# A two-layer hybrid decoder step: one load for the parameters, an earlier up branch in the last chunk, and a final norm by tile

## The reference

```
def rms_norm(x, g):
    y = x * rsqrt(mean(x * x, axis=-1) + EPS)
    return y * g

def conv_ffn(h, prev, w_up, conv_w, conv_b, w_down):
    up = h @ w_up
    a, b = up[..., :D_FF], up[..., D_FF:]          # first and second branch
    c = conv3(concat([prev, a]), conv_w) + conv_b
    return (silu(c) * b) @ w_down

lam = exp(sum(lam_q1 * lam_k1)) - exp(sum(lam_q2 * lam_k2)) + lam_init
y = rms_norm(x, final_g)
```

## Time and profile before

| | us |
|---|---|
| median of 3 runs | 2767.94 (2765.89 to 2774.31) |
| the profiled execution | 2769.99 |
| its span in the profile | 2768.1 |
| TensorE busy in the span | 2548.5 (92%) |
| VectorE, ScalarE, POOL busy | 1422.0 (51%), 739.9 (27%), 804.1 (29%) |
| mean granted clock of TensorE | 0.957 of full speed |

### The profile page before, as it was taken

How to read it: one execution, slowest core, us unless ns; L and a number is a source line. 1 busy time by engine, 2 the same in 40 slices (tenths; PEclk the granted TensorE clock), 3 DMA queues, 4 the chain that set the end, 5 groups by cost and what they waited for, 6 DMA issues and landing times.

```text
span 2768.1 us, 41317 instructions
## 1 busy us (share of the span) xinstructions
PE 2548.5 (92%) x16556; PEld 2386.5 (86%) x16556; DVE 1422.0 (51%) x1845; ACT 739.9 (27%) x1409; POOL 804.1 (29%) x537
## 2 busy tenths in 40 slices
PE   6888888989999999999988898799899999999996
PEld 6776677889999999999887777588899999999995
DVE  6554554364455454444564554543554554544445
ACT  3243333241111111111143344423211111111112
POOL 2254555322221222222121566352222211222220
PEclk8998998999999999999999999899999999999997
DMA  4334444201111111111113454531111111111101
GB/s 142 117 103 130 143 145 140 92 24 46 46 46 46 46 46 46 46 46 47 57 47 104 130 152 137 165 97 47 47 46 46 46 46 46 46 46 46 46 23 62
DMA packets 78359, 205.96 MB, mean 74 GB/s; under 512 B 9146, under 2 KB 31100, under 8 KB 77994
## 3 DMA queue, kind: packets, MB, share of 16 engines
q1 hardware_dynamic: 57018, 136.27, 14.8%
q0 software_dynamic: 18496, 67.58, 7.9%
q10 hardware_dynamic: 2752, 0.80, 0.1%
HBM read 176.63 MB, written 19.98 MB: 71 GB/s over the span
## 4 chain that ended last, share of the span: by engine, by line
PE 83%; DVE 8%; ACT 3%; DMA 2%; POOL 2%; issue 2%; ACTq 1%; DVEq 0%; POOLq 0%; SPq 0%
PE bank L818 35%; PE bank L841 19%; PE bank L484 9%; PE bank L499 5%; PE bank L585 2%; PE bank L560 2%; PE bank L642 1%; DMA arena<-in_cache_v,idx 1%; PE bank L875 1%; DVE arena L1895 1%; PE bank L574 1%; PE bank L664 1%; POOL arena L1164 1%; DVE stat L1927 1%; DVE arena L1780 1%
## 5 line engine op out<-in xcount | busy, mean ns | idle before, releaser
L1247 POOL TENSOR_TENSOR w_lo<-w_raw,w_hi 128x1024 fp32r<-128x1024 f32 x126 | 310.0, 2461 | 1166.8 <-ACT w_hi L1616 1166.8
L2123 DVE TENSOR_TENSOR resid<-bank,resid 128x1032 f32<-128x1032 f32 x336 | 414.2, 1233 | 94.7 <-PE bank L841 94.7
L818 PE MATMUL bank<-act_hi,w_hi 128*128 128x344 f32 x2016 | 434.0, 324 | 3.7 <-DVE arena L2098 3.7
L818 PE MATMUL bank<-act_hi,w_lo 128*128 128x344 f32 x2016 | 428.3, 321 | 0.0
L818 PE MATMUL bank<-act_lo,w_hi 128*128 128x344 f32 x2016 | 426.7, 320 | 0.0
L818 PEld LDWEIGHTS bank<-act_hi,w_hi 128*128 128x128 f32 x2016 | 336.1, 189 | 7.7 <-issue 3.8
L818 PEld LDWEIGHTS bank<-act_hi,w_lo 128*128 128x128 f32 x2016 | 341.2, 189 | 0.0
L818 PEld LDWEIGHTS bank<-act_lo,w_hi 128*128 128x128 f32 x2016 | 338.2, 189 | 0.0
L841 PE MATMUL bank<-gate_hi,w_hi 128*128 128x344 f32 x1008 | 236.8, 343 | 8.3 <-DVE gate_lo L2116 8.3
L484 PE MATMUL bank<-act_hi,w_hi 128*128 128x344 f32 x672 | 227.7, 339 | 14.2 <-DVE arena L1876 14.2
L484 PE MATMUL bank<-act_hi,w_lo 128*128 128x344 f32 x672 | 226.9, 338 | 0.0
(11 more groups left out here) (238 smaller groups left out, 4048.4 us busy)
## 6 DMA issues: line engine op xcount, KB each, us to landing
w_raw<-in_w_up SPq DMA_DIRECT2D x88, 512.0 KB, 3.7
w_raw<-in_w_down SPq DMA_DIRECT2D x44, 512.0 KB, 3.4
w_raw<-in_w_in SPq DMA_DIRECT2D x32, 512.0 KB, 3.3
out<-arena SPq DMA_DIRECT2D x24, 512.0 KB, 3.3
arena<-arena SPq DMA_DIRECT2D x64, 129.0 KB, 2.5
w_raw<-in_w_out SPq DMA_DIRECT2D x16, 448.0 KB, 3.7
mix_spill<-arena SPq DMA_DIRECT2D x12, 516.0 KB, 3.4
arena<-in_x_prompt SPq DMA_DIRECT2D x8, 512.0 KB, 10.5
```

The lines of the kernel that those rows point to most:

```text
L818: ins = pe.matmul(grp(u[0])[:, t, :], w_of(w, l, n, k), x[:, k, cols(t)], start=(k == 0 and n_ == 0), stop=(k == KC - 1 and n_ == 2))
L1247: pool.tensor_tensor(w_lo[:, slot, :], w_raw[:, r % SLOTS, 0:1024], w_hi[:, slot, :].bitcast(F32), ALU.subtract).then_inc(w_lo_done, 1)
L2123: dve.tensor_tensor(tiles(resid[:, m, :]), grp(u[0]), tiles(resid[:, m, :]), ALU.add).then_inc(fg_free[u[0]], 1)
```

## The change

Four edits. Small inputs: they are laid out outside the kernel, so that the parameters come by one load straight into `par`, already turned, the lambda vectors by one broadcast load into the place of the sine table, the page rows by one load. The table's load is put behind lambda's sums on SP. VectorE takes the parameters first, copies tokens from then on, and makes the page rows after the third and the lambda sums after the fourth tile. The exponential moves into the first norm of layer 0 on ScalarE, its use on VectorE (`lambdas_ready`) ahead of that norm's third diagonal.

The diff, cut to its core:

```diff
@@ TensorE
-                if t == 3:
-                    b = claim(pe, ("par",), 6)
-                    pe.wait_ge(params_in, 16 * len(PAR) * DEPTH)
...
-                with pe.Fori(1, FC - 1) as i:
+                with pe.Fori(1, FC - 2) as i:
                     up_unit(ffn_use(l, i, 0), U_FFN + 1, i)
                     chunk(i, i)
-                up_unit(ffn_use(l, FC - 1, 0), U_LAYER - 2)
+                up_unit(ffn_use(l, FC - 2, 0), U_LAYER - 5)
+                up_unit(ffn_use(l, FC - 2, 1), U_LAYER - 4)
+                new_rows(FC - 2)
+                state_rows(FC - 1)
+                up_unit(ffn_use(l, FC - 2, 2), U_LAYER - 3)
                 new_rows(FC - 1)
+                down(FC - 2, U_LAYER - 2, 0, 3)
                 pe.wait_ge(g_lo_done, (l + 1) * FC)
...
+            def turn_tokens(i):
+                pe.wait_ge(y_done, (i + 1) * KC)
+                for n, (at, rows) in enumerate(PARTS):
+                    b = claim(pe, ("out", i, n), 2 * ((i * len(PARTS) + n) % 3))
...
+            sums(ni, 0)
+            sums(ni, 1)
+            turn_tokens(0)
+            sums(ni, 2)
+            turn_tokens(1)
+            turn_tokens(2)
@@ SyncE
                     load_unit(l, h, w_in[l, h])
-                    if l == 0 and h == 0:
-                        sp.dma_start(con[:, CON_SMALL:CON_W], table[:, CON_SMALL:CON_W]).then_inc(rope_in, 16)
...
+                if l == 0:
+                    sp.wait_ge(lam_sum, 1)
+                    sp.dma_start(con[:, CON_SMALL:CON_W], table[:, CON_SMALL:CON_W]).then_inc(rope_in, 16)
                 load_v(0)
...
+            for i in range(NT):
+                for n, (at, rows) in enumerate(PARTS):
+                    freed(sp, ("out", i, n))
+                    first = T_ORDER[i] * TW + at
+                    src, end = x_buf[i * len(PARTS) + n], min(rows, SEQ - first)
+                    sp.dma_start(y_prompt[0, first:first + end, :], src[0:end]).then_inc(y_out, 16)
@@ GpSimd
-            pool.tensor_tensor(nrs[:, :], nrs[:, :], neghalf.broadcast_to([P, QT_N + 1]), ALU.pow).then_inc(norm_rs, 1)
+            for i in range(NT):
+                power(2 * DEPTH, i)
@@ ScalarE
-            for j in range(N_PAGES):
-                act.dma_start(pages[j * GROUPS:(j + 1) * GROUPS, :],
...
+            act.dma_start(par[:, :, 0:PAR_W], params).then_inc(params_in, 16)
+            act.dma_start(lam_in[:, :, :].rearrange("p n x -> p (n x)"),
+                          lambdas.broadcast_to([P, 4 * DEPTH * HEAD_DIM])).then_inc(lam_in_s, 16)
+            act.dma_start(pages[:, :], page_table).then_inc(pages_in, 16)
...
+                if l == 0:
+                    act.wait_ge(lam_sum, 1)
+                    act.activation(lam[:, 4:8], lam[:, 0:4], ACT.Exp).then_inc(lam_exp, 1)
...
+                    act.activation(sq_buf[i % 2][:, 2 * TW * j:2 * TW * (j + 1)].rearrange("p (a b) -> p a b", a=2),
+                                   resid[:, 2 * j:2 * j + 2, tile_of(i)], ACT.Square).then_inc(sq_done, 1)
+                act.wait_ge(sq_done, (ni * NT + i + 1) * PAIRS)
+                for k in range(KC):
+                    act.activation(resid[:, k, tile_of(i)], resid[:, k, tile_of(i)], ACT.Copy,
+                                   scale=p_at("final_g", 0, k)).then_inc(y_done, 1)
...
+            for i in range(NT):
+                b = full(act, ("sums", ni, i))
...
+            for t in range(1, NT * len(PARTS), 2):
@@ VectorE
+                chunk(FC - 2)
+                taps(FC - 1)
+                gate_b(FC - 1, ffn_use(l, FC - 2, 2))
+                add_rows(FC - 2, 3, range(2))
+                low_gate(FC - 1, last_hi, last_lo)
+                add_rows(FC - 2, 3, range(2, KC))
...
             for i in range(NT):
                 for j in range(PAIRS):
                     add_last(i, j)
+                if i:
+                    last_tree(i - 1)
+            last_tree(NT - 1)
...
+            for t in range(0, NT * len(PARTS), 2):
+                last_rows(t)
```

More of the change, by code:

```diff
@@ L1686, in _ @@
+            for t in range(1, NT * len(PARTS), 2):
+                i, n = divmod(t, len(PARTS))
+                rows = PARTS[n][1]
+                act.wait_ge(norm_rs, ni * NT + i + 1)
+                b = full(act, ("out", i, n))
+                act.activation(x_buf[t][0:rows], flat(b)[0:rows], ACT.Copy, scale=nrs[0:rows, t:t + 1]
+                               ).then_inc(bank_free[b], 1)
             act.wait_ge(ks_out_s, 16 * DEPTH * N_HEADS)
@@ new lines, in _, with page_rows @@
+            dve.wait_ge(dve_step, step.n)
+            dve.wait_ge(par_ready, DEPTH)
+            def page_rows():
+                dve.wait_ge(pages_in, 16)
+                page_f, idx_f = small[:, 8:16], small[:, 16:24]
+                step.then(dve.tensor_copy(page_f, pages[:, :]))
+                step.then(dve.tensor_scalar(page_f, page_f, float(GROUPS), c_("group"), ALU.mult, ALU.add))
+                for it in range(DEPTH * N_HEADS):
+                    step.then(dve.tensor_scalar(idx_f, page_f, float(it * GROUPS * N_POOL), None, ALU.add))
+                    ins = dve.tensor_copy(idx[:, it, :], idx_f)
+                    if it < DEPTH * N_HEADS - 1:
+                        step.then(ins)
+                    else:
+                        ins.then_inc(idx_ready, 1)
@@ L1763, in _ @@
[L1763 removed]
+                    dve.wait_ge(lam_in_s, 16)
+                    for n in range(2):
+                        step.then(dve.tensor_tensor(lam_in[:, 2 * n, :], lam_in[:, 2 * n, :], lam_in[:, 2 * n + 1, :],
+                                                    ALU.mult))
+                    step.then(dve.tensor_reduce(lam[:, 0:2], lam_in[:, 0, :].rearrange("p (l d) -> p l d", l=DEPTH),
+                                                AX_X, ALU.add))
```

243 lines of the change are left out of this document (103 added, 140 removed).

## The result

The changed kernel takes 2754.09 us (median of 6 runs, 2750.22 to 2758.7) where the kernel before, timed beside it, takes 2769.31: a ratio of 0.9942, 95% interval 0.993 to 0.9954. Faster, as forecast, but by 15 us and not by 26: 2754 lies above the range of 2733 to 2753. The profiled execution took 2753.09, its span 2751.3.

The account below looks back on a forecast made before the run. TensorE, 83% of the chain that ended last, was taken as the bound, so only its waits or slow stretches could give time back. Gains 10.5 + 5.9 + 6.2 + 3.5 = 26.1 us gave 2743 us, range 2733 to 2753 with three rivals.

Parts of the forecast that it names:

- Start: Start of kernel: fewer small DMAs let VectorE's copies end at 26.0 us; gain 10.5 us, bounds 8.4 to 11.6.
- Last chunk: Each layer's last chunk: the previous down product covers the gate's chain; gain 5.9 us in layer 0, 6.2 in layer 1.
- 2.5, where both operations stand bare: Last chunk: upper bound in us on the net cost of VectorE's gate product and lo part beside eight blocks; 0.5 taken.
- The third rival: End loses what it wins on ScalarE, and VectorE's ten operations stand barer in the last chunks: 2751 us, chance 0.08.
- 2.27 us for the lower clock in layer 1: Last down product: its first 30 matmuls, slowed by the lower clock, return to the upper, counted as 2.27 us gained.
- End: Final norm and output after the last product starts (S): span ends at S + 45; gain 3.5 us, bounds -0.5 to 6.
- the wait for bank 6: End: all three sums share PSUM bank 6; TensorE waits about 7 us until ScalarE reads them after the last gains.
- The first: Start: transfers bound it, parameters and lambda sharing engines with first tokens; copies and weights 2 to 4 us later: 2747, chance 0.13.
- the fifth: Layer 0's first products: TensorE stays at the lower clock, up to 2783 us for 80 us of it; chance 0.03.
- The second: End gives its whole promise, S + 42.5, start at its upper bound 11.6: 2739 us, or 2738; chance 0.13.
- the fourth: Output: 88-row tiles go to eleven engines and load queues unevenly, adding 0.8 us: 2744 us, chance 0.10.
- The sixth: All changed places: pieces move, but other waits of the same length end last, within 8 us of now: 2764, chance 0.03.

Follow-up runs that it names:

- rows_lo: Changed kernel with `new_rows` ahead of the last chunk's first up branch and layer 0's next-layer weight splits held until VectorE's last lo part; 2749.9 us, ratio 0.9919.
- old_last: Changed kernel with each layer's end as before the change, the last chunk's second branch behind the previous chunk's down product; 2755.9 us, ratio 0.9954.
- tree_late: Changed kernel with VectorE's tree over the first tile's squares moved behind the first two of the third tile's four additions; 2753.24 us, ratio 0.9939.

## Why the prediction was wrong

**Start: right.** 10.5 us forecast, 10.7 at the norm's first instruction, 9.7 in the mean of eleven kernels at the first up product. VectorE's chain of copies and page rows ended at 25.95 where 26.0 was counted, and the weights were not later than it. Two roundings in that chain (18 x 0.2 is 3.6 and not 3.7, 4.53 / 4 is 1.13 and not 1.15) come to 0.2 us and change nothing. The changed kernel's profiled run shows 13.2 there, the earliest of the eleven; what it has over the mean is chance and no gain of the change, and the 612.8 of the kernel before is one run too.

**Last chunk: wrong, and this is the step that failed.** "After, the down product of the chunk before, eight blocks in 12.16 us, stands between, and covers the chain", at a net cost of 0.5. The eight blocks took 17.2 and 16.4 us, so the cost was 5.1 and 4.2, about as much as the wait of 4.43 that they were to remove, and TensorE still idled 2.7 and 2.8 us in them, over the 2 us that the prediction named as its sign of being wrong. I walked VectorE's ten operations from the start of the eight blocks on and took for granted that the last chunk's convolution runs as early as in the loop. Two things ahead of that point were not walked. The unrolled code puts `new_rows` behind the first up branch, where the loop has it ahead; through ScalarE's queue this delays VectorE's start by almost 5 us. And the moved work brings VectorE's second tap, and in layer 0 its lo part, beside GpSimd's subtractions. With the order put right and GpSimd away from the lo part (the tap still takes 3.3 us, but early enough) the forecast's mechanism is there: in rows_lo the eight blocks take 12.9 us in both layers, the stretches ahead of the last products fall by 3.4 and 4.0 us (3.9 each forecast), and layer 0's product by another 1.9.
The bound "2.5, where both operations stand bare" did not hold what happened, since it bounded these operations and not when they could start. The third rival named the right place ("ten VectorE operations stand barer in the last chunks") at half the size: it took 4.0 us off there, where 4.5 and 3.7 were missing, and 4.0 off at the end, where 2.4 were. So that its 2751 lies nearest to what came is luck in part.
A second, smaller error sits in the same term: 2.27 us for the lower clock in layer 1. old_last shows that behind the new norm this is not on the path.

**End: mechanism right, size off.** Forecast from S at the upper clock 45, measured 47.4; the wait for bank 6 is there as described. Missing were TensorE's wait for the tree (0.5 to 1.3, tree_late) and the transfers behind the first tile: 17.2 us from the first scaled tile (2734.08) to the end against 16.1 counted. The same 4.23 MB of output kept the 16 DMA engines busy for 59.5% of 20 us on average, 11.9, where it was 56.4% of 19 us, 10.7, before; that fits the 1.1, but why the transfers took longer was not settled.

**The rivals.** The first (transfers at the start) and the fifth (a low clock through layer 0's first products) took nothing that shows: the 10 us of the start are still there at the first up product, and the granted clock is 1.00 from 34 us on. The second (the end gives all it promises) did not come. Of the fourth the way the rows are dealt to the engines is shown, the cost is open. The sixth (other waits end last in the same places) is near to what happened in the last chunks, with waits of 2.7 and 2.8 us in place of 4.43, but not at the start.

## What to carry to other kernels

When a loop's last pass is written out by hand, compare its order with the loop's line by line, and follow each moved instruction through every queue behind it, small stores included. A cover counts only from the time at which the covered chain can start. Before work of VectorE is moved beside work of GpSimd, look whether it takes both inputs from SBUF: the price here was what was left of GpSimd's operation, up to 2.2 us of 2.4.

## What was not expected of the hardware

VectorE stands still for GpSimd. The second taps (128x1048, both inputs in SBUF, the memory that holds the tiles) of the kernel before and of the changed one, grouped by line (count, shortest/median/longest in ns, first and last start):

```profile
L2106 DVE SCALAR_TENSOR_TENSOR arena<-arena,par x44: 1309/1310/1314, 615.4 to 2704.0; 128x1048 f32<-128x1048 f32 x44
```

```profile
L2123 DVE SCALAR_TENSOR_TENSOR arena<-arena,par x44: 1309/1311/3329, 602.1 to 2684.7; 128x1048 f32<-128x1048 f32 x44
```

None of these 44 was slow before; after, the two of the last chunks are. Started 0.35 us after a GpSimd subtraction, they take 3.33 and end 1.11 us after GpSimd does. The lo part: 3.45 us, ending 1.08 after; the changed kernel's in layer 0 2.27, ending 1.10 after. What was left of GpSimd's operation is added, and VectorE's own time follows nearly whole. Additions that read one input from PSUM ran beside it in their usual 1.23. The kernel before shows this too, outside the feed-forward, and there in both orders:

```profile
98.86 1.37 DVE L1895 TENSOR_TENSOR arena<-arena 128x1166 f32<-128x1166 f32 x1
98.92 3.59 POOL L1129 TENSOR_TENSOR w_lo<-w_raw,w_hi 128x1024 fp32r<-128x1024 f32 x1 [8.92 <-ACT w_hi L1286]
```

```profile
100.27 3.47 DVE L1895 TENSOR_TENSOR arena<-arena 128x1164 f32<-128x1164 f32 x1
```

GpSimd, second by 0.06 us, takes 3.59 us instead of 2.4 and ends 2.28 after VectorE's 1.37; VectorE's next, second in its turn, takes 3.47 and ends 1.23 after GpSimd. The Trainium skill says so: SBUF — State Buffer, Who interferes with whom, has a VectorE instruction with two SBUF inputs contend with a GpSimd instruction that reads SBUF, and the second to start blocks until the first is done. These traces agree, in both orders.

A stretch with one program varied by 10 us (599.6 to 609.8) between kernels that differ only behind it. What varies in it was not tried.
